# One level of Strassen's scheme for the expert products of a mixture-of-experts layer in fp32

## The chip, the cores and the metric

The kernel runs on one core of one Trainium2 chip, all in fp32. The metric is the device time of one execution in microseconds. Each core has TensorE (products of a stationary operand, loaded by a weight load, with a moving one), VectorE, ScalarE and GpSimd, each with its own queue, and DMA queues; semaphores order them.

## The reference

One layer of a diffusion trunk, on 128 prompt rows and 1024 latent rows of width D = 1024. A mixer comes first (projection, bidirectional mLSTM, Fourier mixing, output projection); it isn't touched here. Then comes the part at issue:

```
aff = softmax(h @ router_w)                       # 16 experts
gate, idx = top_k(aff.T, cap)                     # cap = 128 latent rows, 16 prompt rows for each expert
a, b = xe @ w1[e], xe @ w3[e]                     # xe = h[idx]: (144, 1024) x (1024, 2048)
ye = (silu(a) * b) @ w2[e] * gate                 # (144, 2048) x (2048, 1024)
y  = scatter-add of ye to the rows idx; x = x + gate2 * y; final RMSNorm
```

The weights of the 16 experts are 384 MiB, each read once.

## The kernel before

**The mixer** (`front`, `mixing`) fills the first 670 us or so. Towards its end SP already issues the first 12 weight transfers.

**The experts** (`experts`, L1699). Work is transposed: features lie on the 128 partitions and the N = 144 chosen rows (128 latent and 16 prompt ones) on the free axis. The weights are the stationary operand, x or h the moving one. `xeT` holds 8 blocks (DT) of 128 features x 144 rows. An expert is 24 transfers of 1 MiB into a ring of 12 slots: 8 pairs of w1 and w3, each of 256 hidden columns, and 8 pieces of w2, each of 256 hidden rows. TensorE goes through a loop of 16 experts:

- up (L1908): for each of 16 blocks f of 128 hidden columns, 8 matmuls for a (w1) and 8 for b (w3) into one PSUM bank of two (`ps_ab`). ScalarE takes silu of a (L1826), VectorE multiplies by b into `hidT` (L2046).
- down (L1921): for each of 8 output blocks d, 16 matmuls over `hidT` into one of two banks (`ps_yy`). ScalarE scales and stores `yT` (L1832) and `yT_p` (L1833) for each d while the next d is summed.

Between experts VectorE transposes the next x (`keep_x`, L2022) and the last y (`keep_y`, L2050), in blocks of 32 x 32; ScalarE and VectorE modulate x; GpSimd gathers x rows one expert ahead and scatter-adds y rows to `stream` (L1801). The order on each engine is written out by hand; nothing is planned at run time. SP loads the ring in order; a slot is free when the product that used it last has counted (`wait_unit`). The last expert's rows don't go through `stream`: TensorE turns them (L1946, L1969) and adds them by a one-hot matrix `hot` (L1941) to the rows read back, and VectorE and ScalarE do the final norm. `stay_awake` (L792) issues idle matmuls in waits. L483 to L1335 are matmuls of the mixer that the prediction uses as measures; L1292 is a transpose and L1252, L1222 and L1269 are plain ones.

Of the kernel before, what the change touches and what calls it, by code (L numbers as in the profile page):

```python
# [23 lines left out]
P = 128  # L24
# [776 lines left out]
def mixing(nc, g):  # L801
# [5 lines left out]
    with ctx:  # L807
# [91 lines left out]
        with nc.Block() as block:  # L899
            @block.sync  # L900
            def _(sp):
# [60 lines left out]
                for p in range(2):  # L962
                    g.load_pair(sp, 0, p)
# [5 lines left out]
                for p in range(2, g.RING // 2):  # L969
                    g.load_pair(sp, 0, p)  # L970
# [728 lines left out]
def experts(nc, g):  # L1699

    N = CAP_L + CAP_P
    ctx = ExitStack()
    with ctx:
# [6 lines left out]
        silu = sb("silu", [P, 2, N])  # L1710
        hT = sb("hidT", [P, FT, N])
# [3 lines left out]
        yS_p = sb("yS_p", [P, P])  # L1715
        normed_quarters, stream_quarters = (x.rearrange("r (q c) -> (r q) c", c=PIECE) for x in (g.normed, g.stream))
        normed_pieces, stream_pieces = (x.rearrange("r (k c) -> (r k) c", c=P) for x in (g.normed, g.stream))
        free_mark = sb("free_mark", [1, 1])
        xs, final_g = sb("xs", [P, TILES, D]), sb("final_g_row", [P, D])
# [10 lines left out]
        ys = g.area[:].rearrange("p (s n) -> p s n", n=D)  # L1730
        pairs = [ctx.enter_context(nc.psum_tensor(f"ps_pair{i}", [P, 2 * 512], F32)) for i in range(4)]
        ps_ab = [pairs[0][:, bass.ts(i, 512)] for i in range(2)]
        ps_yy = [pairs[1][:, bass.ts(i, 512)] for i in range(2)]
# [9 lines left out]
        h_kept, yT_kept, ye_kept, ye_free = sem("h_kept"), sem("yT_kept"), sem("ye_kept"), sem("ye_free")  # L1743
        gathered, scattered, silu_ready = sem("gathered"), sem("scattered"), sem("silu_ready")
        ab_summed, y_done = g.ab_summed, g.y_done
        slots_turned = sem("slots_turned")
        rows_landed, picked, PICKED = sem("rows_landed"), g.x_normed, 2 * TILES
        xe_turned, xT_act, xT_dve = sem("xe_turned"), sem("xT_act"), sem("xT_dve")
        y_turned = sem("y_turned")
        hot_ready, tile_summed, inverted, scaled = sem("hot_ready"), sem("tile_summed"), sem("inverted"), sem("scaled")  # L1750
        gain_loaded, outputs_stored, summed, stream_loaded, tile_added = g.ada_loaded[0:5]
        gain_base, stored_base, summed_base, stream_base, added_base = g.slice_loads[0:5]

        with nc.Block(no_gpsimd_drain=True) as block:
            @block.sync
            def _(sp):
                for p in range(g.RING // 2, 8):
                    g.load_pair(sp, 0, p)
                for q in range(8):
                    g.load_w2(sp, 0, q)  # L1760
                with sp.Fori(1, E) as e:
                    for p in range(8):
                        g.load_pair(sp, e, p)
                    for q in range(8):
                        g.load_w2(sp, e, q)
                sp.dma_start(final_g[:], g.final_g.to_broadcast([P, D])).then_inc(gain_loaded, 16)
                sp.wait_ge(ye_free, E)
                for n, i in enumerate(ORDER):
                    sp.dma_start(xs[:, n], g.stream[bass.ts(i, P), :]).then_inc(stream_loaded, 16)
                for n, i in enumerate(ORDER):  # L1770
                    sp.wait_ge(scaled, n + 1)
                    dst = g.y_prompt_out if i == 0 else g.y_latent_out[bass.ts(i - 1, P), :]
                    sp.dma_start(dst, ys[:, n]).then_inc(outputs_stored, 16)
                sp.wait_ge(outputs_stored, stored_base + 16 * TILES)

            @block.gpsimd
            def _(pool):
# [13 lines left out]
                for e in range(LAST):  # L1791

                    pool.wait_ge(xe_turned, 3 * e + 2)
                    if e == 0:
                        pool.wait_ge(slots_turned, 8)
                    pool.wait_ge(gathered, 80 * e + 16)
                    gather(e + 1)

                    pool.wait_ge(ye_kept, 5 * (e + 1))
                    for c in range(4):  # L1800
                        nc.gpsimd.indirect_dma_start(stream_quarters, bass.IndirectOffsetOnAxis(ap=g.slot_row[:, c, e:e + 1], axis=0), ye[:, c], None,  # L1801
                                                     compute_op=ALU.add).then_inc(scattered, 16)
                    nc.gpsimd.indirect_dma_start(stream_pieces, bass.IndirectOffsetOnAxis(ap=g.slot_row_p[:, e:e + 1], axis=0), ye_p[:], None,  # L1803
                                                 compute_op=ALU.add).then_inc(scattered, 16)
                    pool.wait_ge(scattered, 80 * (e + 1))
# [7 lines left out]
            def _(act):  # L1813
                def keep_x(n):

                    act.wait_ge(xe_turned, 3 * n + 1)
                    for k in range(4):
# [4 lines left out]
                def gated(e):  # L1822
                    for f in range(FT):
                        act.wait_ge(ab_summed, e * FT + (f + 1))
                        act.wait_ge(h_kept, e * FT + (f + 1))
                        nc.scalar.activation(silu[:, f % 2], ps_ab[f % 2][:, 0:N], ACT.Silu).then_inc(silu_ready, 1)  # L1826

                def keep_y(e):
                    act.wait_ge(y_turned, e * 2 + 2)
                    for d in range(DT):  # L1830
                        act.wait_ge(y_done, e * DT + (d + 1))
                        nc.scalar.activation(yT[:, d], ps_yy[d % 2][:, 0:CAP_L], ACT.Copy, scale=g.mod[:, 1, 4, d:d + 1])  # L1832
                        nc.scalar.activation(yT_p[:, d % 4, d // 4], ps_yy[d % 2][:, CAP_L:N], ACT.Copy, scale=g.mod[:, 0, 4, d:d + 1]).then_inc(yT_kept, 1)  # L1833

# [5 lines left out]
                with act.Fori(0, E - 1) as e:  # L1840
                    gated(e)
                    keep_x(e + 1)
                    keep_y(e)
                gated(LAST)
                keep_y(LAST)

                act.wait_ge(ye_free, E)
                act.wait_ge(y_turned, 2 * E + 2)
                act.wait_ge(hot_ready, 1)
                nc.scalar.activation(y_rows[:, HALF:], pairs[0][:, HALF:], ACT.Copy, scale=place[:, 1:2]).then_inc(yT_kept, 1)  # L1850
                for n in range(TILES):
                    if n == 1:
                        act.wait_ge(y_turned, 2 * E + 3)
                        nc.scalar.activation(y_rows_p[:, HALF:], pairs[1][0:CAP_P, HALF:], ACT.Copy,
                                             scale=g.slot_gate_p[0:CAP_P, LAST:E]).then_inc(yT_kept, 1)
                    if n in BY_PE:
                        act.wait_ge(tile_summed, n + 1)
# [9 lines left out]
            def _(pe):  # L1867
# [26 lines left out]
                pe.wait_ge(h_kept, 2)  # L1894
                pe.wait_ge(yT_kept, 2)
                with nc.Fori(0, E, engines=[pe.engine], head_slot={pe.engine: 0}) as e:
                    pe.wait_ge(xT_act, e + 1)
                    pe.wait_ge(xT_dve, e + 1)
                    for f in range(FT):
                        pe.wait_ge(h_kept, e * FT + (f + 1))  # L1900
                        p, c = divmod(f, 2)
                        for w in range(2):
                            s, turn = g.slot(2 * p + w)
                            if c == 0:
                                pe.wait_ge(g.slot_loaded[s], e * 32 + 16 * (turn + 1))
                            unit = g.ring[:, s].rearrange("p (k n) -> p k n", k=DT)
# [3 lines left out]
                        mm.then_inc(ab_summed, 1)  # L1910

                    for d in range(DT):
                        pe.wait_ge(yT_kept, e * DT + (d + 1))
                        for f in range(FT):
                            s, turn = g.slot(16 + f // 2)
                            if d == 0:
                                pe.wait_ge(h_kept, e * FT + (f + 3))
                                if f % 2 == 0:
                                    pe.wait_ge(g.slot_loaded[s], e * 32 + 16 * (turn + 1))
                            unit = g.ring[:, s].rearrange("p (c n) -> p c n", c=2)  # L1920
                            mm = nc.tensor.matmul(ps_yy[d % 2][:, 0:N], unit[:, f % 2, bass.ts(d, P)], hT[:, f], start=(f == 0), stop=(f == FT - 1))  # L1921
                            if d == DT - 1 and f % 2 and f < FT - 1:
                                mm.then_inc(g.w2_used, 1)
                        mm.then_inc(y_done, 1)

                def take_area(n):
                    m = n - 4
                    if m >= 0 and m in BY_PE:
                        pe.wait_ge(scaled, m + 1)
# [7 lines left out]
                def expert_rows(n):  # L1937
                    rows, k = (y_rows_p, CAP_P) if ORDER[n] == 0 else (y_rows, P)
                    pe.wait_ge(hot_ready, n + 2)
# [4 lines left out]
                def turn_rows(d):  # L1944
                    pe.wait_ge(yT_kept, LAST * DT + d + 3)
# [4 lines left out]
                for d in range(DT - 1):  # L1950
                    turn_rows(d)
                turn_rows(DT - 1)
                for h in range(2):
                    stream_rows(BY_PE[0], h)
                for n in range(TILES):
                    take_area(n)
                    if n == 0:
                        pe.wait_ge(ye_kept, 5 * LAST + 1)
                        pe.wait_ge(yT_kept, E * DT + 3)
                    if n == 3:  # L1960
                        pe.wait_ge(ye_kept, 5 * LAST + 2)
                        pe.wait_ge(yT_kept, E * DT + 4)
# [425 lines left out]
```

## Time and profile before

| what | value |
|---|---|
| median of 3 runs | 2221.01 us (2220.08 to 2221.37) |
| profiled execution, its span | 2218.4 us |
| TensorE products busy | 2170.8 us (98%) |
| TensorE weight loads busy | 1860.6 us (84%) |
| VectorE busy | 492.5 us (22%) |
| ScalarE busy | 359.4 us (16%) |
| HBM traffic | 238 GB/s over the span |

The span runs from the first to the last instruction of the profiled execution; the profile gives no other time of it, and what lies around the span is read from the median of the runs. In the page, PE is TensorE's products and PEld its weight loads, which overlap; DVE is VectorE, ACT ScalarE, POOL GpSimd, SP the queue of the plain DMAs. A matmul in fp32 shows as two records of PE and two of PEld. Idle time of an engine names what released it.

### The profile page before, as it was taken

Reading aid. Unit: us, or ns where it says so; the run is one execution under the profiler, and the core shown is the slowest. Engines: PE = TensorE matmul, PEld = TensorE weight load, DVE = VectorE, ACT = ScalarE, POOL = GpSimd, SP = SyncE. Lnnn points to the kernel's source line nnn. Section 1 sums busy time; section 2 is a strip of 40 time slices with the busy share of each in tenths; the row PEclk is TensorE's granted clock in tenths of the full one; section 3 lists DMA queues with packets and bytes.
Section 4 is the critical chain, followed back from the end, with each engine's and each line's share of the span. In section 5 each row is a group of like instructions: output and inputs, shape, how many; then the busy total and the mean of one; then the engine's idle time right before and its main releaser. Section 6 shows DMA issues by size and latency. Waiting matters only on the chain.

```text
span 2218.4 us, 36881 instructions
## 1 busy us (share of the span) xinstructions
PE 2170.8 (98%) x15110; PEld 1860.6 (84%) x15110; DVE 492.5 (22%) x1262; ACT 359.4 (16%) x1029; POOL 255.9 (12%) x260
## 2 busy tenths in 40 slices
PE   7999999999978999999999999999999999999998
PEld 3444444865538999999999999999999999999996
DVE  1111116678872011100111011101111111001103
ACT  1111112433320111111111111101111011111103
POOL 0000000112111021020211202012020210202100
PEclk9999999999989999999999999999999999999999
DMA  9820100934475496977969689696986969769692
GB/s 382 330 105 33 66 33 24 319 135 157 136 258 174 162 360 214 367 214 261 332 224 367 211 292 295 233 364 211 323 259 239 361 212 354 226 249 347 220 382 95
DMA packets 352019, 528.19 MB, mean 238 GB/s; under 512 B 13933, under 2 KB 292573, under 8 KB 348777
## 3 DMA queue, kind: packets, MB, share of 16 engines
q1 hardware_dynamic: 337408, 509.24, 66.1%
q0 software_dynamic: 14336, 18.29, 3.9%
q8 instruction: 25, 0.41, 0.1%
q10 hardware_dynamic: 232, 0.11, 0.0%
q14 instruction: 18, 0.14, 0.0%
HBM read 492.23 MB, written 35.36 MB: 238 GB/s over the span
## 4 chain that ended last, share of the span: by engine, by line
PE 68%; DVE 1%; ACT 0%; issue 0%; DMA 0%; POOL 0%; DVEq 0%; ACTq 0%
PE ps_pair L1908 45%; PE ps_pair L1921 23%; DVE area L2100 0%; DVE area L2105 0%; PE ps_pair L1941 0%; DMA xe_p<-normed,slot_row_p 0%; ACT squares L1862 0%; PE ps_pair L1935 0%; POOL rs L1810 0%; DVE xeT L2034 0%; PE ps_pair L792 0%; PE ps_pair L1946 0%; DVE yS L2110 0%; ACT rs L1864 0%; PE ps_pair L1882 0%
## 5 line engine op out<-in xcount | busy, mean ns | idle before, releaser
L1908 PE MATMUL ps_pair<-xeT,area 128*128 128x144 f32 x8192 | 1006.2, 286 | 1.2 <-DVE xeT L2034 1.2
L1908 PEld LDWEIGHTS ps_pair<-xeT,area 128*128 128x128 f32 x8192 | 1004.6, 190 | 1.5 <-issue 1.5
L1921 PE MATMUL ps_pair<-hidT,area 128*128 128x144 f32 x4096 | 504.4, 286 | 0.0
L1921 PEld LDWEIGHTS ps_pair<-hidT,area 128*128 128x128 f32 x4096 | 502.8, 190 | 0.0
L483 PE MATMUL ps_p<-area,hT 128*128 128x512 f32 x720 | 317.4, 594 | 1.1 <-DMA area<-in_w_in 1.1
L2046 DVE TENSOR_TENSOR hidT<-silu,ps_pair 128x144 f32<-128x144 f32 x256 | 77.9, 304 | 881.3 <-ACT silu L1826 815.8
L483 PEld LDWEIGHTS ps_p<-area,hT 128*128 128x128 f32 x720 | 133.5, 190 | 154.7 <-issue 151.7
L1801 POOL DMA_INDIRECT stream<-ye,slot_row x60 | 94.7, 1578 | 1131.8 <-DVE ye_p L2057 1118.1
L1826 ACT ACTIVATE silu<-ps_pair 128x144 f32<-128x144 f32 x256 | 74.3, 290 | 907.4 <-PE ps_pair L1908 889.3
L1243 PE MATMUL b_z<-w_out,shared 128*128 128x512 f32 x288 | 128.7, 598 | 2.4 <-DVE soft L1591 1.7
L2050 DVE STREAM_TRANSPOSE yS<-yT 128x1024 f32<-128x1024 f32 x15 | 18.7, 1245 | 425.9 <-ACT yT_p L1833 425.9
L1832 ACT ACTIVATE yT<-ps_pair,mod 128x128 f32<-128x128 f32 x128 | 47.0, 367 | 390.0 <-PE ps_pair L1921 390.0
L1243 PEld LDWEIGHTS b_z<-w_out,shared 128*128 128x128 f32 x288 | 53.0, 190 | 64.5 <-issue 59.0
L657 DVE TENSOR_TENSOR pr<-ps_p,area 128x512 f32<-128x512 f32 x45 | 31.1, 691 | 270.9 <-PE ps_p L483 262.2
L1780 POOL DMA_INDIRECT xe<-normed,slot_row x60 | 58.1, 968 | 27.7 <-issue 22.9
L131 POOL TENSOR_TENSOR area<-area,minus_half 128x1 f32<-128x1 f32 x9 | 4.9, 550 | 312.1 <-ACT area L125 312.1
L1833 ACT ACTIVATE yT_p<-ps_pair,mod 128x16 f32<-128x16 f32 x128 | 34.1, 266 | 0.0
L1818 ACT ACTIVATE xeT<-xeS,mod 128x128 f32<-128x128 f32 x60 | 24.7, 482 | 22.9 <-DVE xeS L2022 22.9
L1070 ACT ACTIVATE area<-b_i,cols 128x129 f32<-128x129 f32 x72 | 20.5, 367 | 25.0 <-PE b_i L1222 17.5
L1803 POOL DMA_INDIRECT stream<-ye_p,slot_row_p x15 | 23.3, 1554 | 4.6 <-issue 4.6
L411 PE MATMUL ps_ada<-w_out,area 128*2 128x512 f32 x176 | 23.3, 662 | 0.5 <-DMA w_out<-in_ada_w 0.5
L123 ACT ACTIVATE squares<-x_area 128x1024 bf16<-128x1024 f32 x9 | 9.5, 1057 | 74.8 <-DMA x_area<-in_x_latent 74.7
(320 smaller groups left out, 1056.4 us busy)
## 6 DMA issues: line engine op xcount, KB each, us to landing
area<-in_exp_w SPq DMA_DIRECT2D x384, 1024.0 KB, 12.3
w_out<-in_ada_w SPq DMA_DIRECT2D x22, 1024.0 KB, 8.0
kvo<-pr SPq DMA_DIRECT2D x9, 768.0 KB, 3.3
area<-in_w_in SPq DMA_DIRECT2D x3, 2048.0 KB, 17.7
shared<-kvo SPq DMA_DIRECT2D x12, 512.0 KB, 5.5
qkT_dram<-qkT SPq DMA_DIRECT2D x9, 512.0 KB, 4.6
area<-qkT_dram SPq DMA_DIRECT2D x9, 512.0 KB, 5.9
area<-m_lanes SPq DMA_DIRECT2D x9, 512.0 KB, 6.8
```

Source lines behind the costliest of these rows:

```text
L483: mm = nc.tensor.matmul(ps_p[(par + b) % 2][:], hT[:, par, k], g.w_blocks[b][:, k, W_FROM[b]:W_FROM[b] + 512], start=(k == 0), stop=(k == ...
L657: g.dve.did(nc.vector.tensor_tensor(pr[:, par, b], ps_p[(par + b) % 2][:], g.b_in_row[:, COLS[b]:COLS[b] + 512], ALU.add), block_kept)
L1243: mm = nc.tensor.matmul(b_z[h][:], mixT[:, par, k], g.w_out_sb[:, k, bass.ts(h, 512)], start=(k == 0), stop=(k == DT - 1))
L1780: nc.gpsimd.indirect_dma_start(xe[:, c], None, normed_quarters, bass.IndirectOffsetOnAxis(ap=g.slot_row[:, c, e:e + 1], axis=0)).then_inc( ...
L1801: nc.gpsimd.indirect_dma_start(stream_quarters, bass.IndirectOffsetOnAxis(ap=g.slot_row[:, c, e:e + 1], axis=0), ye[:, c], None, compute_o ...
L1818: ins = nc.scalar.activation(xeT[:, k, 0:CAP_L].rearrange("p (s r) -> p s r", r=QUARTER), xeS[:, :, k], ACT.Identity, scale=g.mod[:, 1, 2, ...
L1826: nc.scalar.activation(silu[:, f % 2], ps_ab[f % 2][:, 0:N], ACT.Silu).then_inc(silu_ready, 1)
L1832: nc.scalar.activation(yT[:, d], ps_yy[d % 2][:, 0:CAP_L], ACT.Copy, scale=g.mod[:, 1, 4, d:d + 1])
L1833: nc.scalar.activation(yT_p[:, d % 4, d // 4], ps_yy[d % 2][:, CAP_L:N], ACT.Copy, scale=g.mod[:, 0, 4, d:d + 1]).then_inc(yT_kept, 1)
L1908: mm = nc.tensor.matmul(ps_ab[f % 2][:, N * w:N * w + N], unit[:, k, bass.ts(c, P)], xeT[:, k], start=(k == 0), stop=(k == DT - 1))
L1921: mm = nc.tensor.matmul(ps_yy[d % 2][:, 0:N], unit[:, f % 2, bass.ts(d, P)], hT[:, f], start=(f == 0), stop=(f == FT - 1))
L2046: nc.vector.tensor_tensor(hT[:, f], silu[:, f % 2], ps_ab[f % 2][:, N:2 * N], ALU.mult).then_inc(h_kept, 1)
```

## The change

The products of an expert go by one level of Strassen's scheme in Winograd's form, which makes 7 products of blocks of half the size where 8 stood. The block axes are the contraction (halves j), the output features (halves i) and the rows (72 and 72, T = 72). The work of an expert is 12 units: 8 up (a pair of slots, w1 and w3, 256 hidden columns), 4 down (two pieces of w2). For each unit VectorE forms four sums of weight quarters of 128 x 1024 elements, two units ahead of TensorE (`first_sum` to `fourth_sum`), one of them in place in the ring, three into `w_sums`. It also forms four sums of x for each expert (`sum_x`), four of h for each pair of units (`sum_h`), joins the products of a and b (`first_a`, `second_a`, `second_b`) and adds up y after the last down unit (`sum_y`). ScalarE copies partial sums out of PSUM (`keep_first`, `keep_bent`, `keep_chain`, `keep_y_parts`), because Winograd's form uses a chained bank at several stages; its scaling of y now runs from SBUF in the next expert (`scale_y`), and weighing of y moves from VectorE to it (`weigh_y`). A slot is free when its whole unit is done (`unit_done`). The rest keeps its arithmetic; some buffers move into space that is dead by then.

```diff
-                    for f in range(FT):
-                        pe.wait_ge(h_kept, e * FT + (f + 1))
-                        p, c = divmod(f, 2)
-                        for w in range(2):
...
-                            for k in range(DT):
-                                mm = nc.tensor.matmul(ps_ab[f % 2][:, N * w:N * w + N], unit[:, k, bass.ts(c, P)], xeT[:, k],
-                                                      start=(k == 0), stop=(k == DT - 1))
...
-                    for d in range(DT):
-                        for f in range(FT):
-                            mm = nc.tensor.matmul(ps_yy[d % 2][:, 0:N], unit[:, f % 2, bass.ts(d, P)], hT[:, f], start=(f == 0), stop=(f == FT - 1))
+                def up_product(u, m, bank, opens):
+                    w, x = stationary(u)[m], x_moving[m]
+                    for c in range(2):
+                        for k in range(DT // 2):
+                            mm = nc.tensor.matmul(bank[:, T * c:T * c + T], w[:, k, bass.ts(c, P)], x[:, k],
+                                                  start=opens and c == 0 and k == 0, stop=c == 1 and k == DT // 2 - 1, skip_group_check=True)
+                def down_product(v, m):
+                    w, h, at = stationary(v)[m], h_moving[m], T * Y_AT[m]
+                    for b in range(4):
+                        for q in range(2):
+                            mm = nc.tensor.matmul(low_bank[b][:, at:at + T], w[:, q, bass.ts(b, P)], h[:, 2 * (v - UP) + q],
+                                                  start=v == UP and m == 1 and q == 0, stop=v == UNITS - 1 and q == 1, skip_group_check=True)
...
+                    for u in range(UP):
+                        pe.wait_ge(w_summed, 4 * UNITS * e + (4 * u + 4))
+                        if u == 0:
+                            pe.wait_ge(x_summed, e * 4 + 4)
+                        if u == 2:
+                            pe.wait_ge(outs_summed, e * 7 + 1)
+                        chained(u, 1).then_inc(product_done, 1)
+                        if u:
+                            pe.wait_ge(joined, JOINS * e + join["a1", u - 1])
+                        up_product(u, 2, plain_bank, True).then_inc(product_done, 1)
+                        if u:
+                            seventh(u - 1)
+                            pe.wait_ge(joined, JOINS * e + join["a2", u - 1])
+                        up_product(u, 5, bent_bank, True).then_inc(product_done, 1)
+                        pe.wait_ge(part_kept, PARTS * e + part[u, 1])
+                        chained(u, 6).then_inc(product_done, 1)
+                        if u:
+                            fourth(u - 1)
+                        pe.wait_ge(part_kept, PARTS * e + part[u, 5])
+                        up_product(u, 3, bent_bank, False).then_inc(product_done, 1)
+                    for v in range(UP, UNITS):
+                        pe.wait_ge(w_summed, 4 * UNITS * e + (4 * v + 4))
+                        pe.wait_ge(h_summed, e * 16 + 4 * (v - UP + 1))
+                        down_product(v, 1)
...
+                        down_product(v, 4).then_inc(unit_done, 1)
...
+                def first_sum(e, n):
...
+                    if n >= 3:
+                        dve.wait_ge(product_done, PRODUCTS * e + product[n - 3, 3])
...
+                    TT(sums_of(v)[0], w21, w22, ALU.add).then_inc(w_summed, 1)
+                def second_sum(e, n):
...
+                    TT(sums_of(v)[1], sums_of(v)[0], w11, ALU.subtract).then_inc(w_summed, 1)
+                def third_sum(e, n):
...
+                    TT(w21, w11, w21, ALU.subtract).then_inc(w_summed, 1)
+                def fourth_sum(e, n):
...
+                    TT(sums_of(v)[2], w12, sums_of(v)[1], ALU.subtract).then_inc(w_summed, 1)
...
+                def body(e, fresh=False, last=False):
+                    for slot in range(UNITS):
+                        n = slot + AHEAD
+                        sums = not (last and n >= UNITS)
+                        if 1 <= slot <= UP:
+                            second_a(e, slot - 1)
+                        if 2 <= slot <= UP + 1:
+                            hidden(e, slot - 2)
+                        if not (last and n > UNITS):
+                            fourth_sum(e, n - 1)
+                        if sums:
+                            first_sum(e, n)
+                        if slot < UP:
+                            first_a(e, slot)
+                        if slot == 0 and not fresh:
+                            sum_y(e - 1)
+                        if slot == 3 and not fresh:
+                            turn_y(e - 1)
+                        if not last and slot == UP:
+                            turn_x(e + 1)
+                        if not last and slot == UP + 1:
+                            prompt_x(e + 1)
+                        if sums:
+                            third_sum(e, n)
+                        if 1 <= slot <= UP:
+                            second_b(e, slot - 1)
+                        if slot in (3, 5, 7, UP + 1):
+                            sum_h(e, (slot - 3) // 2)
+                        if not last and slot == UP + 2:
+                            sum_x(e + 1)
+                        if sums:
+                            second_sum(e, n)
...
-                    for d in range(DT):
-                        act.wait_ge(y_done, e * DT + (d + 1))
-                        nc.scalar.activation(yT[:, d], ps_yy[d % 2][:, 0:CAP_L], ACT.Copy, scale=g.mod[:, 1, 4, d:d + 1])
+                def keep_y_parts(e):
+                    act.wait_ge(unit_done, UNITS * e + UNITS)
+                    nc.scalar.activation(y_part, by_bank[:, :, 0:2 * T], COPY).then_inc(y_part_kept, 1)
+                def scale_y(e, half):
+                    act.wait_ge(outs_summed, 7 * e + 8)
+                    for d in range(DT // 2 * half, DT // 2 * half + DT // 2):
+                        nc.scalar.activation(yT[:, d], y_sum[:, d, 0:CAP_L], COPY, scale=g.mod[:, 1, 4, d:d + 1])
...
+        if not (isinstance(e, int) and g.UNITS * e + v < g.DEEP):
+            sp.wait_ge(g.unit_done, g.UNITS * e + (v - g.DEEP + 1))
```

## Rows read from the trace of the kernel before

**Rows 1.** The page's busy times, with their share of the span.
```profile
PE 2170.8 (98%) x15110; PEld 1860.6 (84%) x15110; DVE 492.5 (22%) x1262; ACT 359.4 (16%) x1029; POOL 255.9 (12%) x260
```

**Rows 2.** The page's chain that ended last, shares by line.
```profile
PE ps_pair L1908 45%; PE ps_pair L1921 23%; DVE area L2100 0%; DVE area L2105 0%; PE ps_pair L1941 0%; DMA xe_p<-normed,slot_row_p 0%; ACT squares L1862 0%; PE ps_pair L1935 0%; POOL rs L1810 0%; DVE xeT L2034 0%; PE ps_pair L792 0%; PE ps_pair L1946 0%; DVE yS L2110 0%; ACT rs L1864 0%; PE ps_pair L1882 0%
```

**Rows 3.** Windows: from:to and length in us, busy by engine, clock, DMA share, GB/s.
```profile
682.28:2187.86 1505.58, 1505.58 (x12290) 1505.58 (x12291) 165.20 (x499) 184.96 (x585) 191.22 (x165) 1.00 0.82 274
...
0.00:60.00 60.00, 47.31 (x179) 19.27 (x180) 7.83 (x24) 8.57 (x16) 1.31 (x6) 1.00 1.00 385
```

**Rows 4.** Groups by line: shapes, count, busy us, mean ns of one, idle before.
```profile
L1908 PE MATMUL ps_pair<-xeT,area 128*128 128x144 f32 x8192 | 1006.2, 286 | 1.2 <-DVE xeT L2034 1.2
L1908 PEld LDWEIGHTS ps_pair<-xeT,area 128*128 128x128 f32 x8192 | 1004.6, 190 | 1.5 <-issue 1.5
L1921 PE MATMUL ps_pair<-hidT,area 128*128 128x144 f32 x4096 | 504.4, 286 | 0.0
```

**Rows 5.** L1941, 512 moving columns: timeline (start, us, engine, line), then its group.
```profile
2190.33 3.60 PE L1941 MATMUL ps_pair<-ye,hot 128*128 128x512 f32 x8
...
L1941 PE MATMUL ps_pair<-ye,hot 128*128 128x512 f32 x32 | 14.5, 596 | 0.8 <-DVE yS L2110 0.8
```

**Rows 6.** Group of the weight loads of 32 columns.
```profile
L492 PEld LDWEIGHTS ps_qk<-hT,area 128*32 128x32 f32 x144 | 3.6, 109 | 6.8 <-issue 6.8
```

**Rows 7.** Timeline rows of short moving operands; their groups; the source view of L579.
```profile
452.99 1.95 PE L1252 MATMUL b_z<-y_prompt,const 128*128 128x128 f32 x16
...
462.23 1.06 PE L1222 MATMUL b_i<-area 128*128 128x129 f32 x8
...
498.18 1.04 PE L1292 MATMUL b_z<-const,shared 128*128 128x128 f32 x8
...
397.21 0.63 PEld L573 LDWEIGHTS ps_qk<-const,area 36*128 36x128 f32 x9
...
399.08 0.44 PE L579 MATMUL ps_ada<-x_area 64*128 64x72 f32 x2
...
399.08 0.30 PEld L579 LDWEIGHTS ps_ada<-x_area 64*128 64x128 f32 x2
...
L1292 PE MATMUL b_z<-const,shared 128*128 128x128 f32 x48 | 6.2, 273 | 0.0
...
L1292 PEld LDWEIGHTS b_z<-const,shared 128*128 128x128 f32 x48 | 5.4, 141 | 0.0
...
L573 PEld LDWEIGHTS ps_qk<-const,area 36*128 36x128 f32 x9 | 0.6, 138 | 0.1
...
L579 PEld LDWEIGHTS ps_ada<-x_area x2: 183/185/187, 399.1 to 399.2; 64*128 64x128 f32 x2
L579 PE MATMUL ps_ada<-x_area x2: 272/300/327, 399.1 to 399.3; 64*128 64x72 f32 x2
```

**Rows 8.** Groups of VectorE: sums of 144 and 1152 elements, a transpose.
```profile
L2046 DVE TENSOR_TENSOR hidT<-silu,ps_pair 128x144 f32<-128x144 f32 x256 | 77.9, 304 | 881.3 <-ACT silu L1826 815.8 <-issue 65.5
L2050 DVE STREAM_TRANSPOSE yS<-yT 128x1024 f32<-128x1024 f32 x15 | 18.7, 1245 | 425.9 <-ACT yT_p L1833 425.9
...
L734 DVE TENSOR_TENSOR x_area<-area,x_area 64x1152 f32<-64x1152 f32 x1 | 1.4, 1351 | 0.0
```

**Rows 9.** Timeline at the start and at the end of the experts.
```profile
682.28 17.90 PE L1908 MATMUL ps_pair<-xeT,area 128*128 128x144 f32 x144 [1.22 <-DVE xeT L2034]
...
2187.86 0.37 ACT L1832 ACTIVATE yT<-ps_pair,mod 128x128 f32<-128x128 f32 x1 [3.39 <-PE ps_pair L1921]
2188.13 0.27 ACT L1833 ACTIVATE yT_p<-ps_pair,mod 128x16 f32<-128x16 f32 x1
```

**Rows 10.** A stretch at half clock: its window, the timeline row, the group.
```profile
401.74:404.40 2.66, 2.66 (x13) 2.66 (x13) 1.39 (x4) 1.86 (x6) 1.17 (x2) 0.50 1.16 280
...
401.74 2.86 PE L1269 MATMUL b_n<-shared,area 128*128 128x129 f32 x12
...
L1269 PE MATMUL b_n<-shared,area 128*128 128x129 f32 x24 | 4.4, 351 | 0.0
```

More of the change, by code:

```diff
@@ L962, in _ @@
                 for p in range(2):
[L963 removed]
+                    g.load_unit(sp, 0, p)
                 turn(TILES, 1, TILES // 2)
@@ new lines, in sums_of, with stationary @@
+        def sums_of(v):
+            rows = DT // 2 if v < UP else 2
+            return [w_sums[:, v % 3, n].rearrange("p (k n) -> p k n", k=rows) for n in range(3)]
+        def stationary(v):
+            (w11, w12), (w21, w22) = quarters(v)
+            s1, s2, s4 = sums_of(v)
+            return {1: w11, 2: w12, 3: s4, 4: w22, 5: s1, 6: s2, 7: w21}
+        x_of = {(j, h): xeT[:, DT // 2 * j:DT // 2 * j + DT // 2, T * h:T * h + T] for j in range(2) for h in range(2)}
+        x_moving = {1: x_of[0, 0], 2: x_of[1, 0], 3: x_of[1, 1], 4: x_sums[:, 2], 5: x_sums[:, 0], 6: x_sums[:, 1], 7: x_of[0, 1]}
@@ new lines, in second_b, with hidden @@
+                def second_b(e, u):
+                    dve.wait_ge(part_kept, PARTS * e + part[u, 5])
+                    dve.wait_ge(product_done, PRODUCTS * e + product[u, 7])
+                    TT(b_second, b_part[u % 2], chain_bank[u % 3][:, 0:N], ALU.add).then_inc(joined, 1)
+                def hidden(e, u):
+                    h = [hT[:, u, i].rearrange("p c n -> p (c n)") for i in range(2)]
+                    dve.wait_ge(silu_ready, UP * e + (silu_base + u + 1))
+                    dve.wait_ge(joined, JOINS * e + join["b2", u])
+                    TT(h[1], a_of[u % 2][:, N:2 * N], b_second, ALU.mult).then_inc(h_kept, 1)
+                    dve.wait_ge(unit_done, UNITS * e + (u + 1))
+                    TT(h[0], a_of[u % 2][:, 0:N], chain_bank[u % 3][:, 0:N], ALU.mult).then_inc(h_kept, 1)
@@ L2057, in keep_y @@
-                    nc.vector.tensor_scalar(ye_p[:], yS_p[:], g.slot_gate_p[:, bass.ds(e, 1)], None, ALU.mult).then_inc(ye_kept, 1)
-                keep_x(0)
-                with dve.Fori(0, E - 1) as e:
-                    for f in range(FT):
-                        hidden(e, f)
-                    keep_x(e + 1)
-                    keep_y(e)
                 def place_rows():
@@ new lines, in _ @@
+                turn_x(0)
+                prompt_x(0)
+                for k in (2, 3, 6, 7):
+                    dve.wait_ge(slots_turned, 5 + k // 2)
+                    did(TS(xeT[:, k, 0:CAP_L], ps_turned[k // 2][:, bass.ts(k % 2, P)],
+                           g.mod[:, 1, 2, k:k + 1], g.mod[:, 1, 3, k:k + 1], ALU.mult, ALU.add))
+                settle()
+                sum_x(0)
+                fourth_sum(0, 0)
+                first_sum(0, 1)
+                third_sum(0, 1)
+                second_sum(0, 1)
```

406 lines of the change are left out of this document (253 added, 153 removed).

## The prediction, made before the changed kernel was run

> **What bounds the kernel now.** I read first the page's busy shares [rows 1]: TensorE's products are busy 98% of a span of 2218.4 us, its weight loads 84%, VectorE 22%, ScalarE 16%. An engine at 98% can still be waiting for somebody, so the chain of waits comes next [rows 2]: 45% and 23% of the span lie in two lines of TensorE, the up products L1908 and the down products L1921, and no other line reaches 1%. The window over the experts [rows 3] gives that stage its length, 1505.58 us, with TensorE busy in all of it at a granted clock of 1.00 (2.4 GHz), VectorE in 165 and ScalarE in 185 us. No DMA, no eviction and no handshake between engines has a share there: the weights arrive at 274 GB/s, while the kernel's first 60 us [rows 3] show 385 GB/s, so the transfers have room too.
>
> The groups [rows 4] count 8192 + 4096 = 12288 product records, twice the matmuls of the code (16 experts x 384): an fp32 matmul is two passes, each with a weight load of its own. 1505.58 / 12288 = 122.5 ns for a pass. Beside each pass of 144 moving columns runs the load of the next 128 stationary columns. The load is busy as long as the product (1505.58 us each [rows 3]), since each follows the other in step. That is the point to look at: a pass costs the longer of two things, and which of them sets the 122.5 ns must be found before the columns are cut.
>
> **What a pass costs, by its columns.** A merged row of n passes lasts (n-1) periods and one duration. For 512 moving columns [rows 5]: (3.60 - 0.596) / 7 = 429 ns. From 144 to 512 columns that is (429 - 122.5) / 368 = 0.833 ns a column, so down to 144 columns the moving side sets the period. Extended to 128 columns the line gives 109.2 ns, to 72 columns 62.5 ns.
>
> The load side: loads of 32 and 128 stationary columns last 109 and 190 ns [rows 4, 6], so 81 / 96 = 0.84 ns a column and 128 x 0.84 = 108 ns for a full load over a fixed part of 82 ns that overlaps. That is above 62.5. Three rows say that such a load can't be hurried [rows 7]. Plain passes of 128 columns: (1.95 - 0.273) / 15 = 111.8 ns; of 129 columns, (1.06 - 0.273) / 7 = 112.4. Transposes of the same 128 columns, whose loads are shorter (141 ns, one pass over the data): (1.04 - 0.273) / 7 = 109.6, which is the moving line's value. So the plain pass of 128 columns already stands 2 ns above the moving line: there the load has taken over. The trace even holds the new shape once: L579 is an fp32 matmul with 128 stationary and 72 moving columns, two passes. Its loads start 0.30 - 0.187 = 0.113 us apart, and its products end 0.44 - 0.327 = 0.113 us apart, not 0.0625. And the transposes L573 move only 36 columns: (0.63 - 0.138) / 8 = 61.5 ns apart, where 36 columns would take 30; their load, 138 - 82 = 56 ns, sets the pace with 5.5 ns on top.
>
> The row shows 113 ns between passes of 72 columns [rows 7]. The Trainium skill (TensorE: Matmul & The Clock Gate, Back-to-back issue gap) gives a lone gap as the moving columns over the clock plus 2.5 ns, and by that rule alone, with the two cycles a column that the rows show, a pass would take 62.5 ns and the stage 21504 x 0.0625 = 1344 us. The same page (LDWEIGHTS) gives a load as its columns over 1.2 GHz, 106.7 ns for 128 whatever moves, which would make the stage 21504 x 0.1067 = 2294 us at least. The trace agrees with the second, at 111.7 to 113 ns.
>
> **The change part by part.** Products. Before, one unit of two weight blocks takes 2 x 2 x 8 = 32 matmuls of 144 columns; after, 7 products x 2 x 4 = 56 of 72 columns. Down: 128 matmuls of an expert become 4 units x 7 x 4 x 2 = 224. So 672 in place of 384 for each expert, and 16 x 672 x 2 = 21504 passes in place of 12288. The moving columns fall by 1/8 (56 x 72 = 4032 against 32 x 144 = 4608), but the stationary columns to be loaded rise by 3/4 (56 against 32 loads). With the period set by the load: 21504 x 0.1118 = 2404 us in place of 1505.6, **+898.5 us**. Lower bound of the period 0.84 x 128 = 107.5 ns (2312 us), upper bound the load's 108 plus the 5.5 ns of L573, 114 ns (2451 us). I take 111.8, between the rows of 128 and 129 columns, of which there are most and which last longest; the single pair of 72 is 1 ns away.
>
> Weight sums on VectorE. 48 sums of 1024 elements for each expert. The nearest row is 1152 elements from SBUF at 1351 ns, beside 304 ns for 144 [rows 8]: 1047 / 1008 = 1.04 ns an element, so a sum of 1024 takes 1.22 us, 48 of them 58.6 us. Joins and products of silu: 8 units x 5 x 0.304 = 12.2; h sums 16 x 0.304 = 4.9; x and y sums 11 of 288 elements at 0.455 = 5.0; two transposes of 1.245 and the prompt's small operations, 3.6 in all [rows 8]. Together 84.3 us an expert, beside 1344 x 0.1118 = 150.3 us of TensorE. It costs nothing under that cover; were the cover gone (TensorE at 84.0 us), VectorE would be the bound. Even at twice the price for each weight sum it would be 143 us, still hidden; a gain is excluded, as VectorE isn't on the path.
>
> Waits inside a unit. TensorE now waits for copies and joins five or six times a unit. A product is 16 passes, 1.79 us. The shortest cover is for product 4 of the last unit, which needs second_b on VectorE. Queued before that one there are, from the end of product 2 on, first_a (0.3) and third_sum (1.2), in unit 3 also turn_y (1.5): 3.0 us, and product 7 of TensorE ends 1.79 us after product 2. So second_b is done about 3.4 us after product 2, and product 4 begins after 7, 5 and 6, at 5.4 us: 2 us to spare. The copies on ScalarE, 0.37 us each by the nearest row [rows 9], have one whole product as cover; behind them in its queue in unit 1 and 2 stand the eight scalings of y (2.5 us), with 3.6 us to spare before product 3. I take nothing; a loss of 0.1 us at each of 5 waits would be 16 x 8 x 5 x 0.1 = 64 us, and a gain is excluded, since TensorE has no idle time to give back. The queue of SP issues the same 384 transfers, each pair now released by unit_done; at 150 us an expert instead of 94 they need 171 GB/s instead of 274. POOL's gathers and scatters are the same in number, one expert later.
>
> Start of the stage. Before, TensorE starts 0.34 us after the last of x, at 682.28 [rows 9]. Now VectorE puts three weight sums (3.7 us) where 0.9 us of memsets stood, which end 0.25 us after xe_p lands, and then four x sums (1.9 with their waits) and fourth_sum (1.2) before TensorE's first wait is met: +3.3 us. TensorE stands 4.5 us instead of 1.2, and if its clock falls, a stretch of 3.4 us at 1.2 GHz loses 1.7. I take 5, between 3 and 7.
>
> End. Before, only one eviction of y is left at the end, 0.37 + 0.27 us [rows 9]. Now a copy of 576 elements (0.7), seven sums (3.2 and 0.5 of handoffs) and 16 scalings in a row (8 x 0.64 = 5.1) stand between the last product and the last transpose: 9.5, +8.9 us. TensorE's rows afterwards (L1941, 3.60 us for 8 [rows 5]) would cost that much more at half clock; I take 3 of it: 12, between 9 and 15.
>
> **Sum.** 2218.4 - 1505.6 + 2404.1 + 5 + 12 = 3133.9 us of span. The median of the runs shown, 2221.0, is 2.6 above the profiled span, so 3136.5, say **3137 us**.
>
> **The rivals.** (1) The load doesn't bind at 72 columns, and the moving columns do; this is the side on which the kernel gets faster. Place: each pass of the experts; price 62.5 ns, 84.0 us an expert, where VectorE's 84.3 us take over: 16 x 84.3 = 1349 us, and in the up units up to 100 us more, since sums and joins of a unit (4 x 1.22 + 5 x 0.304 + 0.6 = 7.0 us) just equal its products (112 x 0.0625 = 7.0). That gives 2082 to 2183, about 2130 us. It decides once a load takes under 108 ns. For it: before, loads are hidden whole. Against it: L579, L573 and the 2 ns between plain passes and transposes. (2) The handoffs bind: each of the 640 waits of the up units costs a full handoff of some 0.3 us, +190 us, 3330 us. For it: six waits a unit between three engines where there was one kind. Against it: the 2 us to spare worked out above. (3) The clock falls to 1.2 GHz in the stage, as the moving columns fill only half of it. Price from a stretch at half clock [rows 10]: (2.86 - 0.351) / 11 = 228 ns a pass, 21504 x 0.228 = 4903 us, some 5640 us in all. Against it: TensorE would still be issued a pass every 112 ns without a break, and in the first 60 us, with its products busy in 47 and its loads in 19 of them, the clock was 1.00 [rows 3].
>
> **How the numbers follow.** Forecast 0.89, rival (1) 0.04, rival (2) 0.05, rival (3) 0.02. The forecast's bounds are 2312 to 2451 us of passes with 12 to 22 at the edges, 3040 to 3189, and up to 64 us of waits on top, 3253; with part of rival (2) I set the range at 3045 to 3290 us. Two cases lie outside, with 0.06, and the rest of rival (2). 0.2% is 4.4 us, about what can be told from no change here: slower 0.95, same 0.01, faster 0.04.
>
> **What would show it.** In the changed kernel: 21504 product records of 128x72 with periods of 111 to 114 ns and loads of 190 ns, the load's busy time near that of the stage (about 2400 us) and above the products' 62 ns of moving; a stage of 150 us an expert; VectorE near 55% busy in it; clock 1.00. A period near 62 ns, or TensorE idle behind VectorE, would prove the forecast wrong; idle time behind joins or copies beyond 60 us in sum would prove the claim of cover wrong.

## The result, and the profile after

The changed kernel takes 5317.92 us (median of 4 runs, 5317.3 to 5318.18) against 2221.13 us (4 runs, 2220.08 to 2221.37): **2.394 times as long**, 95% interval 2.391 to 2.398. Slower was forecast, but 3137 us, with 3290 as the upper end. The page of the kernel after, the lines that answer to [rows 1, 2, 4] and the clock line of the 40 slices:

```profile
span 5315.5 us, 58641 instructions
PE 5258.0 (99%) x24326; PEld 4944.9 (93%) x24326; DVE 1562.5 (29%) x2706; ACT 493.1 (9%) x1422; POOL 274.1 (5%) x260
...
PEclk9999955555555555555555555555555555555555
...
PE ps_pair L2008 49%; PE ps_low L2020 29%; PE ps_low L2008 8%; DVE area L2356 0%; DVE area L2361 0%; DMA xe<-normed,plain_row 0%; PE ps_pair L2088 0%; PE ps_low L2083 0%; ACT squares L1970 0%; PE ps_low L2077 0%; PE ps_low L1998 0%; POOL rs L1876 0%; DVE w_sums L2145 0%; ACT xeT L1944 0%; ACT const L1909 0%
...
L2008 PE MATMUL ps_pair<-xeT,area 128*128 128x72 f32 x5120 | 1122.6, 421 | 4.6 <-DVE w_sums L2145 4.1
L2008 PEld LDWEIGHTS ps_pair<-xeT,area 128*128 128x128 f32 x5120 | 1109.1, 333 | 5.9 <-issue 5.8
...
L2128 DVE TENSOR_TENSOR w_sums<-area 128x1024 f32<-128x1024 f32 x192 | 234.2, 1220 | 842.4 <-PE ps_low L2020 842.4
```

Every share looks better than before: TensorE 99% busy, its loads 93%, nothing else near. The busy shares don't show the loss. The fives of the clock line do, and so do the mean durations, 333 ns for a load that took 190 [rows 4]. The windows (columns as in rows 3) over the experts, then over the end:

```profile
686.01:5275.80 4589.79, 4589.23 (x21504) 4588.04 (x21504) 1227.24 (x1933) 314.99 (x963) 205.96 (x163) 0.50 0.29 91
5276.00:5315.50 39.50, 26.95 (x64) 11.38 (x64) 22.32 (x30) 17.96 (x46) 5.56 (x9) 0.80 0.29 120
```

21504 passes in 4589.79 us are 213.4 ns each, at a granted clock of 0.50 (1.2 GHz) from first to last. The difference in span, 5315.5 - 2218.4 = 3097.1 us, is the stage (4589.8 - 1505.6 = 3084.2), its start (686.01 - 682.28 = 3.7) and its end (39.7 - 30.5 = 9.2). TensorE's waits hardly exist:

```profile
PE ps_pair L2008 <- DVE w_sums L2145: 4.1, 1, 4.1
PE ps_pair L2088 <- ACT yT_p L1915: 4.1, 1, 4.1
```

These two (us in all, times, longest) are the longest around the stage: one wait before its first product, one after its last. In between TensorE is idle for 4589.79 - 4589.23 = 0.56 us. The timeline of the first products shows the idle time ahead of them and their pace, (4.33 - 0.421) / 18 = 217 ns, from the start:

```profile
686.01 4.33 PE L2008 MATMUL ps_pair<-xeT,area 128*128 128x72 f32 x19 [4.06 <-DVE w_sums L2145]
```

### The profile page after: what moved, and what is told of

The parts are those of the page before. It is cut to its first block, busy times and chain, and to the rows that moved or that the text cites. A ratio compares the mean times of both kernels' runs of the same rounds, so it can differ in the third digit from the quotient of the medians.

```text
span 5315.5 us, 58641 instructions
## 1 busy us (share of the span) xinstructions
PE 5258.0 (99%) x24326; PEld 4944.9 (93%) x24326; DVE 1562.5 (29%) x2706; ACT 493.1 (9%) x1422; POOL 274.1 (5%) x260
## 4 chain that ended last, share of the span: by engine, by line
PE 87%; DVE 0%; ACT 0%; issue 0%; DMA 0%; POOL 0%; DVEq 0%; ACTq 0%
PE ps_pair L2008 49%; PE ps_low L2020 29%; PE ps_low L2008 8%; DVE area L2356 0%; DVE area L2361 0%; DMA xe<-normed,plain_row 0%; PE ps_pair L2088 0%; PE ps_low L2083 0%; ACT squares L1970 0%; PE ps_low L2077 0%; PE ps_low L1998 0%; POOL rs L1876 0%; DVE w_sums L2145 0%; ACT xeT L1944 0%; ACT const L1909 0%
## 5 line engine op out<-in xcount | busy, mean ns | idle before, releaser
L2008 PE MATMUL ps_pair<-xeT,area 128*128 128x72 f32 x5120 | 1122.6, 421 | 4.6 <-DVE w_sums L2145 4.1
L2008 PE MATMUL ps_pair<-x_sums,w_sums 128*128 128x72 f32 x3584 | 791.2, 421 | 0.0
L2008 PEld LDWEIGHTS ps_pair<-x_sums,w_sums 128*128 128x128 f32 x3584 | 779.9, 333 | 0.0
L2020 PE MATMUL ps_low<-hidT,area 128*128 128x72 f32 x3072 | 681.9, 421 | 0.0
L2020 PEld LDWEIGHTS ps_low<-hidT,area 128*128 128x128 f32 x3072 | 670.7, 333 | 0.0
L2008 PE MATMUL ps_pair<-xeT,w_sums 128*128 128x72 f32 x2048 | 463.5, 421 | 0.0
L2008 PEld LDWEIGHTS ps_pair<-xeT,w_sums 128*128 128x128 f32 x2048 | 452.2, 333 | 0.0
L2020 PE MATMUL ps_low<-gate,w_sums 128*128 128x72 f32 x2048 | 450.2, 421 | 0.0
L2020 PEld LDWEIGHTS ps_low<-gate,w_sums 128*128 128x128 f32 x2048 | 444.6, 333 | 0.0
L2008 PE MATMUL ps_pair<-x_sums,area 128*128 128x72 f32 x1536 | 347.6, 421 | 0.0
```

The source lines that it names most:

```text
L2008: mm = nc.tensor.matmul(bank[:, T * c:T * c + T], w[:, k, bass.ts(c, P)], x[:, k], start=opens and c == 0 and k == 0, stop=c == 1 and k == ...
L2020: mm = nc.tensor.matmul(low_bank[b][:, at:at + T], w[:, q, bass.ts(b, P)], h[:, 2 * (v - UP) + q], start=v == UP and m == 1 and q == 0, st ...
```

## The experiments

Each was one profiled run beside one run of the kernel before on the same chip (2220.2 to 2221.2 us); the differences read from them are 9 us and more, the largest 3 ms. Windows start after the first passes, so that they show the granted clock of the stretch.

**1. Start at full clock.** After some 4 us of waiting, TensorE's first pass had met a half clock. In a_warm it comes from idle matmuls instead:

```diff
+                pe.wait_ge(w_summed, 4)
+                pe.wait_ge(x_summed, 4)
+                stay_awake(nc, g, bent_bank, 4, 12)
                 with nc.Fori(0, E, ...) as e:
```

> The changed kernel with one edit: TensorE waits for the first x sums and weight sums and then does 12 idle matmuls of 512 columns (24 passes of 0.43 us, some 10 us) directly before the loop over the experts, so that the first pass of the experts runs at a granted clock of 1.00. Theory A (a stream of passes with 72 moving columns can't keep the clock, however it starts): the clock falls to 0.50 soon after the loop begins, passes come 213 ns apart, and the time is about 5328 us. Theory B (the stage only kept the clock that it began with, since TensorE had just stood idle): the clock stays at 1.00, passes come 111.8 ns apart, 3145 us. Theory C (VectorE's sums beside the products draw the clock down): as A here.

Measured: 5196.7 us. Windows of the first expert and of the rest, and the timeline around the seam (start, us, engine, line):

```profile
700.00:849.00 149.00, 149.00 (x1337) 149.00 (x1336) 73.33 (x112) 14.97 (x41) 5.53 (x5) 1.00 0.49 160
851.00:5150.00 4299.00, 4298.64 (x20144) 4297.38 (x20145) 1148.63 (x1816) 298.92 (x921) 196.76 (x155) 0.50 0.29 91
```
```profile
847.27 1.95 PE L2020 MATMUL ps_low<-gate,area 128*128 128x72 f32 x16
851.04 1.26 PE L2008 MATMUL ps_pair<-xeT,area 128*128 128x72 f32 x8 [1.81 <-issue]
```

None of the three theories. The clock held at 1.00 for all of the first expert (1337 passes in 149 us, 111.4 ns each), with VectorE's sums beside it, so theories A and C fall; then the clock fell and didn't return, so B alone isn't enough. What lies at the seam is 1.81 us in which TensorE stands idle and waits for nothing but issue, at the loop's jump back.

**2. Narrow passes without Strassen.** b_w72, b_w96 and b_w112 are the kernel before with the moving operand cut and four idle matmuls ahead of the loop, so that the stage starts at full clock. The rows beyond 72, 96 or 112 are left out:

```diff
-  matmul(ps_ab[f % 2][:, N * w:N * w + N], unit[:, k, bass.ts(c, P)], xeT[:, k], ...)
+  matmul(ps_ab[f % 2][:, N * w:N * w + 72], unit[:, k, bass.ts(c, P)], xeT[:, k, 0:72], ...)
-  matmul(ps_yy[d % 2][:, 0:N], unit[:, f % 2, bass.ts(d, P)], hT[:, f], ...)
+  matmul(ps_yy[d % 2][:, 0:72], unit[:, f % 2, bass.ts(d, P)], hT[:, f, 0:72], ...)
```

> The kernel before, with the moving operand of all expert matmuls cut from 144 to 72 columns (the other rows are left out), and four idle matmuls of 512 columns ahead of the loop. 12288 passes as before; no Strassen, no weight sums. Theory A: clock 0.50, passes 213 ns apart, 2218 - 1506 + 12288 x 0.2133 + 3 = 3337 us, so half the moving columns take half as long again. Theories B and C: clock 1.00, passes 111.8 ns apart (the load), 12288 x 0.1118 = 1374 us, 2091 us in all.

> The kernel before with 96 of the 144 moving columns (the other rows are left out). The load binds at either clock: 2091 us if the clock holds at 1.00, 3337 us if it falls. Theory A says that it may fall, and less surely than with 72; theories B and C 2091.

> The kernel before with 112 of the 144 moving columns (the other rows are left out). All theories: clock 1.00, passes 111.8 ns apart, bound by the load, 2091 us; if the clock falls even here, 3337 us.

Measured: 2098.8, 2099.6 and 2098.6 us; the window of b_w72:

```profile
685.00:2070.00 1385.00, 1378.90 (x12305) 1375.47 (x12304) 165.96 (x500) 186.13 (x587) 189.74 (x163) 1.00 0.89 298
```

Three widths, one time: from 72 to 112 columns the load alone sets the pass. 1378.90 / 12305 = 112.1 ns, where the moving line would give 62.5 at 72 columns. Theory A is out a second time: here 72 columns kept the full clock for 1.4 ms. This kernel's turns have short pauses too, 0.3 to 0.7 us; the first of the fourteen:

```profile
831.85 1.86 PE L1923 MATMUL ps_pair<-hidT,area 128*128 128x72 f32 x15 [0.30 <-DMA area<-in_exp_w]
```

```profile
701.50:3103.00 2401.50, 2398.41 (x21479) 2398.27 (x21478) 1220.89 (x1935) 315.50 (x963) 207.17 (x160) 1.00 0.55 173
```

The whole price of the half clock, 5317.9 - 3140.5 = 2177 us, hangs on about 4 us of waiting before the loop and 1.8 us at its jump.

**4. Wide passes behind each jump.** a_rewarm adds to a_warm, at the head of each expert:

```diff
                 with nc.Fori(0, E, ...) as e:
+                    stay_awake(nc, g, plain_bank, 4, 10)
                     for u in range(UP):
```

> The kernel a_warm, with 10 idle matmuls of 512 columns at the head of each expert as well, behind the jump back. Theory D: if the jump's idle stretch costs the clock, the wide passes win it back, and the narrow ones of the expert hold it: 16 x 20 x 0.429 = 137 us of idle matmuls on top of 3146, 3283 us, and up to 16 x 7 = 112 us more where the first of them run at half clock. Theory A': as a_hint under it, some 5400 us.

Measured: 3311.2 us. The pauses of 1.5 to 2.0 us are all there (15 of them), and the window from 705 to 3260 us has a mean clock of 1.00:

```profile
705.00:3260.00 2555.00, 2528.30 (x21724) 2451.66 (x21723) 1218.88 (x1928) 315.17 (x963) 207.18 (x160) 1.00 0.52 163
```

Taken one by one, the pauses differ. Behind thirteen of them the clock is 1.00 in the first 3 us. Behind two (rows from 1662.01 and 2948.80 us) it fell within those 3 us, to a mean of 0.67, and came back under the idle matmuls, whose row took 10.52 us instead of 8.82:

```profile
1501.20 8.82 PE L792 MATMUL ps_pair<-const 128*128 128x512 f32 x20 [1.89 <-issue]
...
1662.01 10.52 PE L792 MATMUL ps_pair<-const 128*128 128x512 f32 x20 [1.96 <-issue]
```

So a pause of this length doesn't always cost the clock, and where it did, wide passes won it back, which the narrow ones of a_warm never did. Why thirteen cost nothing isn't shown.

**5. Start cold.** b_w72_cold and b_cold are b_w72 and the kernel before, with `pe.wait_ge(gathered, 96)` ahead of the loop.

> The kernel b_w72 (72 of the 144 moving columns, the other rows are left out), with one edit: TensorE waits ahead of the loop for the gather of the second expert's rows, some 8 us of standing idle, so that the first pass of the experts runs at half clock. Theory D: the clock stays at 0.50 to the end of the experts, 12288 x 0.2133 = 2621 us, 3345 us in all, against 2098.8 of b_w72. Theory A' or any in which the start is of no account: about 2110 us.

> The kernel before, all 144 columns, with the same wait ahead of the loop. Theory D: passes that are bound by their moving columns win the clock back within microseconds, 2221 + 8 + 3 to 7 = 2232 to 2236 us. A rival in which the start decides for every stream: 12288 x 0.240 = 2949 us, 3670 us in all.

Measured: 3346.9 us and 2229.8 us. The windows of b_w72_cold, then of b_cold, and the first row of each in the experts, in the same order:

```profile
691.00:3310.00 2619.00, 2619.00 (x12277) 2619.00 (x12277) 165.24 (x499) 184.86 (x584) 187.13 (x160) 0.50 0.48 158
```
```profile
697.00:2190.00 1493.00, 1493.00 (x12190) 1493.00 (x12189) 164.96 (x498) 183.85 (x581) 187.11 (x160) 1.00 0.83 276
```
```profile
690.96 3.26 PE L1911 MATMUL ps_pair<-xeT,area 128*128 128x72 f32 x14 [5.62 <-DMA xe_p<-normed,slot_row_p]
...
690.24 5.97 PE L1909 MATMUL ps_pair<-xeT,area 128*128 128x144 f32 x33 [9.43 <-DMA xe_p<-normed,slot_row_p]
```

This is theory D on the kernel before, with no weight sums and no other thing of the change: one wait costs the 72-column stream 1248 us, and the 144-column stream 9 us. The waits aren't equally long: b_w72_cold stands idle for 5.62 us behind its idle matmuls, b_cold, which has none, for 9.43 us instead of 1.22 [rows 9], so nearly all of its 9 us is the wait itself.

**6. Which widths come back.** The same wait ahead of b_w112 and b_w96.

> The kernel before with 112 of its 144 moving columns (the other rows are left out), and the wait of 8 us ahead of the loop, as b_w72_cold (3346.9 us, clock 0.50 to the end) and b_cold (2229.8 us, clock back within 10 us). Theory D: open where between 72 and 144 columns a stream wins the clock back; if it does, 2098.6 + 12 = 2111 us, otherwise 3347.

> As b_w112_cold, with 96 of the 144 moving columns (the other rows are left out): 2112 us if the stream wins the clock back, 3347 if it does not.

Measured: 2108.5 and 2106.1 us. Both streams won the clock back within the first 10 us; b_w96_cold at its start and afterwards:

```profile
690.00:694.00 4.00, 4.00 (x20) 4.00 (x21) 0.00 (x0) 0.00 (x0) 0.00 (x0) 0.55 0.02 4
...
697.00:2070.00 1373.00, 1366.37 (x12212) 1364.48 (x12212) 164.86 (x498) 183.60 (x581) 186.85 (x160) 1.00 0.90 300
```

Of the widths tried, 96, 112 and 144 came back and 72 did not.

**7. Widen for nothing.** a_pad is the changed kernel without idle matmuls and hint, but with 128 moving columns in its up products; the surplus lands in PSUM columns that nobody reads:

```diff
-  mm = nc.tensor.matmul(bank[:, T * c:T * c + T], w[:, k, bass.ts(c, P)], x[:, k], ...)
+  mm = nc.tensor.matmul(bank[:, bass.ts(c, P)], w[:, k, bass.ts(c, P)], x[k], ...)   # x[k] is 128 wide
-  nc.scalar.activation(a_part, chain_bank[u % 3][:, 0:N], COPY)...
+  nc.scalar.activation(pair(a_part), halves(chain_bank[u % 3]), COPY)...             # and six reads like it
```

> The changed kernel without idle matmuls and without the hint, but with the moving operand of the up products widened from 72 to 128 columns: the 56 more are whatever lies behind the wanted ones, and their results go to columns of the bank that nobody reads. The down products keep 72. The load sets the period of both, so at full clock the wider passes cost nothing. Theory D: wide passes win back the clock after the cold start and after every jump back, narrow ones hold it in between: 3127 us (3146 less the idle matmuls and what they wait for) + 15 jumps x 1.8 us, up to 16 x 7 us more at half clock, so 3150 to 3260. A rival in which only idle matmuls of 512 columns, or passes bound by their moving columns, win it back: 5318 us, as the changed kernel.

Measured: 3182.5 us. Windows of the first expert, of the first jump back and of the second expert, and the first row of products:

```profile
681.00:838.00 157.00, 151.76 (x1396) 151.35 (x1388) 84.00 (x128) 17.27 (x46) 11.56 (x10) 1.00 0.47 156
838.20:841.60 3.40, 3.40 (x16) 3.40 (x17) 0.00 (x0) 0.00 (x0) 0.00 (x0) 0.52 1.01 322
842.00:990.00 148.00, 148.00 (x1327) 147.89 (x1325) 77.04 (x121) 19.40 (x61) 14.22 (x11) 1.00 0.54 171
```
```profile
686.28 3.83 PE L2021 MATMUL ps_pair<-xeT,area 128*128 128x128 f32 x32 [3.81 <-DVE w_sums L2158]
```

Each of the fifteen pauses at the jump (1.5 to 2.1 us) still costs the clock, which is 0.50 to 0.55 in the first 3 us behind each; behind the first, 3.4 us later it is back. The wider passes cost nothing: 1327 passes in 148 us are 111.5 ns, as with 72 columns. With 78% more moving columns in two thirds of the passes the kernel is 2135 us faster. Not all of that is shown to be the padding's, for its start wasn't cold: after a wait of 3.81 us the clock was still 1.00, where 4.06 us had cost it in the changed kernel, and why isn't shown. Against a_warm, which had its first expert at full clock too, a_pad is 5196.7 - 3182.5 = 2014 us faster; that is the recovery behind the jumps.

**8. Halve the rows, without Strassen.** b_halves splits each matmul of the kernel before, the down products likewise, with four idle matmuls ahead of the loop and the hint at its jump:

```diff
+  for r in range(2):
+      matmul(ps_ab[f % 2][:, N * w + 72 * r:N * w + 72 * r + 72], unit[:, k, bass.ts(c, P)], xeT[:, k, 72 * r:72 * r + 72], ...)
```

> The kernel before with every expert matmul done as two of 72 moving columns, with the same stationary operand loaded for each; all the work is done, without Strassen's scheme and without weight sums. Four idle matmuls before the loop and the hint at the jump back, as in a_hint. 24576 passes of 72 columns. Theory D with the load as the bound: 24576 x 0.1118 = 2748 us, 3463 us in all, so that 7 products for 8 are worth 3072 passes or 343 us, and halving the rows costs 1242. If the moving columns set the pace: about 2250 us. If the clock falls: 24576 x 0.2133 = 5242, about 5960 us.

Measured: 5808.3 us; a miss. First expert and part of the second, then the seam:

```profile
680.00:855.00 175.00, 175.00 (x1588) 172.85 (x1580) 10.09 (x31) 12.93 (x39) 4.74 (x5) 1.00 0.31 105
857.00:1200.00 343.00, 341.38 (x1601) 341.34 (x1601) 13.29 (x38) 13.67 (x40) 20.66 (x16) 0.50 0.30 96
```
```profile
858.66 3.69 PE L1911 MATMUL ps_pair<-xeT,area 128*128 128x72 f32 x16 [1.62 <-issue]
```

The hint that had removed the pause in a_hint left one of 1.62 us at the first jump here, and the clock went as theory D has it. Why the hint was of no use in this loop (3072 load and product records a turn, 2688 in a_hint) wasn't tried. What 7 products for 8 gain and what halving the rows costs, at full clock, comes out by estimate only: 24576 x 0.1117 = 2745 us of passes against 2402 for 21504, so about 343 us gained by 7 for 8 and 1240 lost by halving. The two measured kernels differ by 5808.3 - 5317.9 = 490 us, but b_halves had its first expert at full clock. Its 1536 passes there saved some 1536 x (0.2134 - 0.1117) = 156 us, so at half clock throughout the difference would be about 646 us, near the 3072 x 0.2134 = 656 us of the passes saved.

## Why the prediction was right or wrong

**The step that failed** is in "start of the stage": "TensorE stands 4.5 us instead of 1.2, and if its clock falls, a stretch of 3.4 us at 1.2 GHz loses 1.7". The idle time was sized rightly (4.06 us), the fall was foreseen, and the return was taken for granted. In the kernel before, the streams that met a half clock moved 128 columns and more, so no row showed a narrow one that stays there. What a fall costs depends on the stream behind it: 9 us for b_cold, the wait included, 1248 for b_w72_cold, and 2177 for this kernel, in place of 1.7. A warm start alone wouldn't have saved the forecast: a_warm lost the clock at its first jump, a wait that the prediction doesn't have, and took 5196.7 us.

**Rival (3)** came true, at 0.02. It was priced at 228 ns a pass and some 5640 us; the pass took 213.4, so 5318. Its place was right. What stood against it was misread: in the first 60 us, at a clock of 1.00 with loads busy in only 19 of them [rows 3], 138 of the 179 passes have moving operands of 512 columns, so they said nothing of a narrow stream. And the rival was argued as a state that narrow passes bring about; they keep either state, as a_warm and b_w72 show for the full clock.

**The load as the bound** was right. 111.8 ns was forecast; at full clock a_hint has 2398.41 / 21479 = 111.7 ns, b_w72 112.1. With the clock held, the forecast of 3137 us met 3140.5, in part by luck: 12 us of a_hint are its idle matmuls, and without them it would be about 3128, since start, passes and end each took 1 to 4 us less than forecast. At half clock the pass is 213.4 ns, 2 x 106.7, so the few ns on top are gone there. Rival (1), that the moving columns set the pace, is excluded by the equal times of 72, 96 and 112 columns.

**The cover of VectorE** held: 1220.89 / 16 = 76 us an expert in a_hint against 84 estimated and 150 of TensorE. A weight sum took 1.22 us, as estimated from 1152 elements. **The waits inside a unit** cost nothing: over the experts of a_hint TensorE is busy in 2398.41 of 2401.50 us, so rival (2) is out.

**A wait that wasn't listed.** The jump back. The prediction counted semaphores only, and a turn of TensorE's loop grew from 768 passes to 1344, each a load and a product. The page's instruction queue, before and after:

```profile
q8 instruction: 25, 0.41, 0.1%
```
```profile
q8 instruction: 210, 3.44, 0.3%
```

Columns: packets, MB, share. After the change 185 more packets of code came. That the new ones belong to the jumps fits their number, but wasn't shown one by one. a_hint has 196 packets and no pause, so the hint hid the fetch and didn't save it. At full clock the 15 pauses come to 26.7 us (a_rewarm). In the changed kernel as it ran, at half clock, they don't show: 0.2 us of waiting for issue in the whole stage. But a_warm shows that one of them would have cost it the clock even after a warm start. The Trainium skill (Runtime: NRT & Kernel Launch, Instruction fetch mechanics) gives TensorE's instruction memory as 2048 instructions, refilled in blocks of 256, and says that a taken branch whose target isn't in the current two-page window waits for a fetch of that page. With each record counted as one instruction, the trace fits the 2048 as the limit: 2 x 768 = 1536 records a turn went without such a pause, 2 x 1344 = 2688 with one of 1.5 to 2.1 us at full clock. It doesn't fit two pages of 256, since 1536 records are more than those.

**Start and end**: +3.7 us, where 3.3 was forecast without the clock; +9.2, where 12 was forecast. The seven sums of y took 2.65 us as a row, since sums of 0.45 us start 0.37 us apart, and the end ran at a mean clock of 0.80.

## What to carry to other kernels

A pass with a fresh stationary operand of 128 columns (a matmul in fp32 has two) costs the same 112 ns at full clock whether it moves 72 or 128 columns. Count loads, not multiplications: a scheme that saves an eighth of the products and halves their moving side pays 3/4 more loads. And when moving operands get narrow, look for every place where TensorE stands idle, the jump of a long loop among them: the 72-column stream here kept the full clock but did not win it back. Where the load is the bound, wider moving operands, up to 128 columns here, are free and brought it back. No version of the scheme came near the kernel before: 3140.5 us at best, against 2221.

## What the runs showed of the hardware that was not expected

TensorE 100% busy by the profile, at half clock for 4.6 ms (clock 0.50 in the window from 686 to 5276 us). The same stream at full clock for 2.4 ms (a_hint). Which of the two it was, a few microseconds of idle time decided: 4.06 us before the loop of the changed kernel, 1.81 us at the jump of a_warm; 0.3 to 0.7 us, fourteen times, cost b_w72 nothing. Length alone doesn't settle it: 3.81 us before the loop of a_pad cost nothing, and the pauses at the jump, 1.5 to 2.1 us, cost the clock fifteen times out of fifteen in a_pad and twice out of fifteen in a_rewarm. At half clock, streams of 96, 112 and 144 moving columns came back within 10 us, and one of 72 never did in 2619 us. What decides whether a pause costs the clock stays open, and whether the hint alone would save the changed kernel after its cold start wasn't tried.
